# The output of all eight token tiles is summed in PSUM banks by TensorE, the residual rows included; the squares and the final product read the banks

## The reference

```python
def reference(x, ...):
    ...
    x = x + gt1 * hybrid_mixer(h, ...)
    h = rmsnorm(x, g_norm2[l]) * (1.0 + sc2) + sh2
    x = x + gt2 * moe(h, router_w, router_b, exp_w1[l], exp_w3[l], exp_w2[l])
    return rmsnorm(x, g_final)

def moe(h, ...):
    ...
    out = jnp.einsum('nk,nkd->nd', weights, y_assign)   # two expert rows per token, weighted

def rmsnorm(x, g):
    y = x * lax.rsqrt(jnp.mean(x * x, axis=-1, keepdims=True) + EPS)
    return y * g
```

## Time and profile before

| what | us |
|---|---|
| time, median of 3 runs | 1066.58 (1065.75 to 1068.83) |
| the profiled execution, its own time | 1064.69 |
| its span | 1062.9 |
| last expert product ends, from the span's start | 1013.5 |
| first tile of expert rows is there | 1023.6 |
| last `finish` ends | 1058.65 |

### The profile page before, as it was taken

One profiled execution on the slowest core, in us unless ns is written; L12 is line 12 of the kernel. 1 busy time (PEld: TensorE's weight loads), 2 busy tenths in 40 slices (PEclk: granted clock), 3 DMA queues, 4 the chain that ended last, 5 costly groups with the idle time before them and its releaser, 6 DMA issues.

```text
span 1062.9 us, 12951 instructions
## 1 busy us (share of the span) xinstructions
PE 982.5 (92%) x5014; PEld 675.1 (64%) x5014; DVE 546.6 (51%) x858; ACT 353.8 (33%) x525; POOL 133.7 (13%) x130
## 2 busy tenths in 40 slices
PE   3799999999999999985899999999999999999853
PEld 2478988888889688874664755656475565545321
DVE  2589734514663356654773546447354554625126
ACT  4521124422223443331743424243251422522022
POOL 1100000001210001113122202222220020210001
PEclk9899999999999999995899999999999999999977
DMA  9838611111203272428999999999999999999975
GB/s 367 290 124 308 249 41 40 40 40 41 98 24 140 84 291 101 119 90 266 326 359 390 403 428 427 427 425 429 426 426 427 427 426 426 427 426 428 406 302 220
DMA packets 52319, 295.82 MB, mean 278 GB/s; under 512 B 10889, under 2 KB 23194, under 8 KB 35874
## 3 DMA queue, kind: packets, MB, share of 16 engines
q1 hardware_dynamic: 43682, 274.00, 65.1%
q0 software_dynamic: 7424, 16.80, 4.1%
q10 hardware_dynamic: 1152, 4.19, 1.0%
HBM read 278.03 MB, written 25.33 MB: 285 GB/s over the span
## 4 chain that ended last, share of the span: by engine, by line
PE 77%; DMA 10%; DVE 6%; ACT 2%; issue 1%; DVEq 1%; POOL 1%; ACTq 0%; SPq 0%; POOLq 0%
PE bank L1151 9%; PE bank L1132 8%; DMA place_dt_float<-in_exp_w_dram 8%; PE bank L1127 5%; PE bank L1121 5%; PE bank L1157 4%; PE bank L1124 4%; PE bank L822 4%; PE bank L824 4%; PE bank L823 4%; PE bank L827 4%; PE bank L828 4%; PE bank L829 4%; PE bank L996 2%; PE bank L999 2%; PE bank L1002 2%
## 5 line engine op out<-in xcount | busy, mean ns | idle before, releaser
L1428 ACT CAST place_dt_float32r<-place_dt_float 128x4096 fp32r<-128x4096 f32 x32 | 115.7, 3615 | 128.6 <-DMA place_dt_float<-in_exp_w_dram 99.8
L1988 DVE TENSOR_TENSOR place_dt_float32r<-place_dt_float,place_dt_float32r 128x4096 fp32r<-128x4096 f32 x32 | 141.4, 4417 | 26.6 <-ACT place_dt_float32r L1428 26.6
L1151 PE MATMUL bank<-place_dt_float,arena 128*128 128x512 f32 x256 | 113.7, 597 | 0.8 <-issue 0.8
L1132 PE MATMUL bank<-place_dt_float,tail_dt_float 128*64 128x512 f32 x512 | 113.4, 595 | 0.0
L723 POOL DMA_INDIRECT y_dram<-arena,slot_i x24 | 61.0, 2543 | 411.7 <-DVE arena L1999 392.6
L827 PE MATMUL bank<-low_r 128*128 128x256 f32 (+1 forms) x320 | 93.8, 293 | 0.0
L829 PE MATMUL bank<-low_r 128*128 128x256 f32 (+1 forms) x320 | 90.8, 284 | 0.0
L828 PE MATMUL bank<-low_r 128*128 128x256 f32 (+1 forms) x320 | 90.7, 284 | 0.0
L641 POOL TENSOR_TENSOR stats<-stats,half 128x1 f32<-128x1 f32 (+1 forms) x34 | 26.3, 775 | 460.8 <-DVE stats L1480 434.0
L1151 PEld LDWEIGHTS bank<-place_dt_float,arena 128*128 128x128 f32 x256 | 47.3, 190 | 56.0 <-issue 54.6
L1132 PEld LDWEIGHTS bank<-place_dt_float,tail_dt_float 128*64 128x64 f32 x512 | 35.3, 137 | 72.8 <-issue 72.8
(11 more groups left out here) (272 smaller groups left out, 1536.5 us busy)
## 6 DMA issues: line engine op xcount, KB each, us to landing
place_dt_float<-in_exp_w_dram SPq DMA_DIRECT2D x96, 2048.0 KB, 23.4
arena<-in_w_ada_dram SPq DMA_DIRECT2D x24, 1024.0 KB, 9.2
low<-in_w_in_dram SPq DMA_DIRECT2D x11, 1024.0 KB, 5.5
arena<-y_dram SPq DMA_DIRECT2D x8, 1024.0 KB, 7.4
arena<-in_x_dram SPq DMA_DIRECT2D x2, 2048.0 KB, 12.2
wout_dt_float<-in_w_out_dram SPq DMA_DIRECT2D x2, 2048.0 KB, 7.8
arena<-in_x_dram SPq DMA_DIRECT2D x8, 512.0 KB, 3.6
x_dram<-arena SPq DMA_DIRECT2D x8, 512.0 KB, 2.6
```

Source lines behind the costliest of these rows:

```text
L1132: mm = pe.matmul(out_[rows_, :], x[:, k, rows_], w[:, k, :], start=(k == 0), stop=(k == KD - 1))
L1151: mm = pe.matmul(bank[5 + j][:], hT_sb[:, k, :], ws[0][:, k, cols], start=(k == 0), stop=(k == KF - 1))
L1428: act.copy(part_hi[0 if kind == "w1" else 1], alias[F32][n % SLOTS]).then_inc(S["w_hi"], 1)
L1988: TT(alias[F32R][n], alias[F32][n], part_hi[j].bitcast(F32), ALU.subtract).then_inc(S["w_lo"], 1)
```

## The change

PE now forms the whole output of all eight tiles in the banks. `residual(t)` puts the residual rows there with an identity matrix as the stationary operand (two products of 128x512, the first of their banks' sums); the four products with the routing weights are added to them. Tile t uses banks 2*(t%4) and 2*(t%4)+1, so four tiles are under way at once. The residual products of tiles 0 to 3 stand ahead of everything else; that of tile t+1, for tiles 4 to 7, stands behind the products of tile t and waits until tile t-3 is finished. ACT squares the two halves straight from the banks, each with its own sum. DVE adds the two sums (and EPS) in one small instruction and multiplies the banks by the norm and `gfin` into `acc`, in two halves. DVE's passes over the expert rows and its additions of the banks are gone. `w_diag` now has 16 matrices in place of 10.

```diff
-        by_pe = (1, 2, 3, 5, 6)
-        w_diag = F.take(len(by_pe), 2, P)
+        w_diag = F.take(TILES, 2, P)
+        out_bank = lambda t, h: bank[2 * (t % 4) + h]
+        ss_half = mv
...
+            def residual(t):
+                wait(pe, S["fin_out"], t - 3)
+                for h in range(2):
+                    pe.matmul(out_bank(t, h)[:], ident, acc[:, t, h * HT:(h + 1) * HT], start=True, stop=False)
+
+            pe.wait_ge(S["y_ready"], PASSES)
+            pe.wait_ge(S["early_ld"], 32)
+            for t in range(4):
+                residual(t)
             pe.wait_ge(S["h2_act"], TILES + 1)
-            for n, t in enumerate(by_pe):
+            for t in range(TILES):
                 pe.wait_ge(*y_landed(t))
-                if n >= 2:
-                    pe.wait_ge(S["fin_acc"], by_pe[n - 2] + 1)
                 for h in range(2):
                     for k in range(2):
-                        mm = pe.matmul(bank[2 * (n % 2) + h][:], w_diag[:, n, k, :], yy[:, t, k * D + h * HT:k * D + (h + 1) * HT],
-                                       start=(k == 0), stop=(k == 1))
+                        mm = pe.matmul(out_bank(t, h)[:], w_diag[:, t, k, :], yy[:, t, k * D + h * HT:k * D + (h + 1) * HT],
+                                       start=False, stop=(k == 1))
                 mm.then_inc(S["out_mm"], 1)
+                if 4 <= t + 1 < TILES:
+                    residual(t + 1)
...
             for t in range(TILES):
-                act.wait_ge(S["fin_acc"], t + 1)
-                act.activation(sq_junk, acc[:, t, :], ACT.Square, accum_out=ssf[:, t:t + 1])
+                act.wait_ge(S["out_mm"], 2 * TILES + t + 1)
+                for h in range(2):
+                    act.activation(sq_junk[:, h * HT:(h + 1) * HT], out_bank(t, h)[:], ACT.Square, scale=D ** -0.5,
+                                   accum_out=ss_half[:, t, h:h + 1])
                 act.drain().then_inc(S["fin_ss"], 1)
                 if t:
                     store(t - 1)
...
-            def mean_of_tile(t):
+            for t in range(TILES):
                 dve.wait_ge(S["fin_ss"], t + 1)
-                mean_sq(ssf[:, t:t + 1], msf[:, t:t + 1], D, S["fin_ms"])
-
-            def finish(t):
+                STT(msf[:, t:t + 1], ss_half[:, t, 0:1], EPS, ss_half[:, t, 1:2], ALU.add, ALU.add).then_inc(S["fin_ms"], 1)
                 dve.wait_ge(S["fin_rs"], t + 1)
-                STT(acc[:, t, :], acc[:, t, :], rsf[:, t:t + 1], gfin, ALU.mult, ALU.mult).then_inc(S["fin_out"], 1)
-
-            for t in range(TILES):
-                if t in by_pe:
...
+                for h in range(2):
+                    cols = slice(h * HT, (h + 1) * HT)
+                    ins = STT(acc[:, t, cols], out_bank(t, h)[:], rsf[:, t:t + 1], gfin[:, cols], ALU.mult, ALU.mult)
+                ins.then_inc(S["fin_out"], 1)
```

More of the change, by code:

```diff
@@ L168, in build @@
         ss1, ms1, rs1 = (stat(TILES) for _ in range(3))
-        ssf, msf, rsf = ss1, ms1, rs1
+        msf, rsf = ms1, rs1
         mv = stat(2 * TILES).rearrange("p (t two) -> p t two", two=2)
@@ L387, in build @@
                   "ov_sil", "ov_hid", "ov_htr", "ov_hT", "ov_y", "ov_ysb", "ov_sc", "ov_free", "gp_passed", "dve_passed",
-                  "early_ld", "fin_acc", "fin_ss", "fin_ms", "fin_rs", "fin_out"):
+                  "early_ld", "fin_ss", "fin_ms", "fin_rs", "fin_out"):
             S[n] = sem(n)
@@ L1202, in _ @@
                     mm.then_inc(S["ov_y"], 1)
+                pe.wait_ge(S["ov_ysb"], OVER)
+            def residual(t):
[6 more added lines that the diff above has]
+                residual(t)
             pe.wait_ge(S["h2_act"], TILES + 1)
-            for n, t in enumerate(by_pe):
+            for t in range(TILES):
                 pe.wait_ge(*y_landed(t))
-                if n >= 2:
-                    pe.wait_ge(S["fin_acc"], by_pe[n - 2] + 1)
                 for h in range(2):
                     for k in range(2):
-                        mm = pe.matmul(bank[2 * (n % 2) + h][:], w_diag[:, n, k, :], yy[:, t, k * D + h * HT:k * D + (h + 1) * HT],
-                                       start=(k == 0), stop=(k == 1))
+                        mm = pe.matmul(out_bank(t, h)[:], w_diag[:, t, k, :], yy[:, t, k * D + h * HT:k * D + (h + 1) * HT],
+                                       start=False, stop=(k == 1))
                 mm.then_inc(S["out_mm"], 1)
+                if 4 <= t + 1 < TILES:
+                    residual(t + 1)
         @block.scalar
@@ L1442, in _ @@
             act.wait_ge(S["y_mm"], PASSES)
-            for n, t in enumerate(by_pe):
+            for t in range(TILES):
                 for k in range(2):
-                    ins = act.activation(w_diag[:, n, k, :], ident, ACT.Identity, scale=top_w[:, t, k:k + 1])
+                    ins = act.activation(w_diag[:, t, k, :], ident, ACT.Identity, scale=top_w[:, t, k:k + 1])
             ins.then_inc(S["h2_act"], 1)
```

## The result

The changed kernel takes 1070.47 us (median of 20 runs, 1067.62 to 1073.04), the kernel before 1066.12 us in the same series. The ratio is 1.0041, 95% interval 1.0032 to 1.0050: slower by 4.4 us (3.4 to 5.3). The forecast was 1071.2 us and 0.43%.

A forecast was written before the change was run, and what follows sets the result against it. DVE's loop bounds the tail before, PE after: start 1024.8, plus 34.3 us of products, 0.24 us and 3.96 us puts the last `finish` at 1063.3, 4.6 us later: 1071.2 us, 0.43% slower, range 1068.5 to 1073.6.

The forecast's parts named there:

- The bound: Tail from about 1036 us: DVE and its loop with ACT and POOL set the pace before; PE after the change.
- The price of a product: PE's products in the tail: 0.858 us each at full clock, 0.429 us for each of two records; 40 take 34.3 us.
- Rival D: PE's records follow each other faster in a long run; below 0.371 us the kernel is faster, at 0.248 us 1055.6; chance 0.06.
- Rival E: Residual products of tiles 4 to 7 cost nothing, taking 6.9 us off: 2.3 us faster, 1064.3 us; chance 0.10.
- The start: PE's first eight residual products wait for the gain vector until 1016.2, take 6.9 us plus 1.7 us, and end at 1024.8.
- the half clock: PE's start on the residual products: half speed for 3.4 us, costing 1.7 us.
- rival B: First residual products run at full clock or end by 1023.64, saving 1.2 us: 3.4 us slower, 1070.0 us; chance 0.22.
- A: The forecast itself: PE bounds the tail, with half clock for 3.4 us at its start; 1071.2 us; chance 0.50.
- Behind PE: Steps after PE's last product: two squares 1.4 us, read to `finish` 1.26 us, `finish` 1.3 us; together 3.96 us.
- The 0.24 us: Delay between the end of PE's last product at 1059.1 and ACT seeing it at 1059.3.
- The sum: End of the tail: last `finish` at 1063.3 instead of 1058.65, 4.6 us later; on the median 1066.58 this gives 1071.2 us.
- the hold of ACT's queue: Kernel before, ACT's first store: 1.76 us on the chain at 1037.66, read as the end of a longer hold.

The follow-up runs named there:

- `own_sem`: Changed kernel with the last norm's gain vector on its own semaphore, so PE's first residual products wait for the residual rows alone: 1069.05 us, ratio 1.0051; again 1069.03 us, 1.0027.
- the third series: Last four kernels on one chip: changed kernel again (1071.60 us), gain vector on its own semaphore, five added products before the residuals, and the kernel before with later stores.
- `filler`: Changed kernel with five more identity products behind PE's last expert product, to keep PE busy until the residual products: 1069.17 us, ratio 1.0024; again 1069.89 us, 1.0037.

## Why the prediction was right

**The bound.** It was read as DVE and its loop before and PE after. Both are shown: 8.5 us of DVE work cost 5.5 us before (a stretch of 40.6 against 35.0) and nothing after (38.15 in both), and four tiles' residual products done twice cost 6.5 us.

**The price of a product.** 0.858 us, taken from two DVE starts 3.43 us apart, held for the 40 products from tile 0 on: the changed kernel's chain has 1.72, 3.43 and 13.73 us for four, eight and 32 records. The 34.3 us from tile 0 to the last product are there to the tenth (1027.28 on the chain to 1061.62 in the timeline). Rival D is out: over 80 records the spacing stayed at 0.429 us. The Trainium skill has two figures for this, in "TensorE: Matmul & The Clock Gate", section "Back-to-back issue gap". If a record is two passes, which no run here shows, the measured spacing agrees with the isolated gap of some 216 ns for each pass and not with the sustained 131 ns. Rival E is out: the late residual products cost their full price.

**The start.** This is the term that was sized worst. It was put at 1024.8 us, 1.2 us behind tile 0's landing. In the changed kernel's first profile PE goes on to tile 0 only at 1027.28: the gain vector landed at 1017.75, not 1016.2, since it was issued 1.56 us later than in the kernel before (988.47 against 986.91), and the half clock took 4.6 us, not 3.4. Tile 0's rows, 10.1 us behind the last expert product as elsewhere, would by an estimate have let PE go on at about 1023.7, so this start costs 3.6 us. In the four profiles of variants with the same wait it costs nothing (rival B): PE stood still for 2.5 to 2.9 us, about as long as the forecast had it, but went on at full clock. Single executions thus show 3.6 us (A, longer than forecast) or nothing (B), and none the 1.2 us of the forecast. In the median the comparison with `own_sem` in the third series prices the start at 2.6 us. One reading of the rows was wrong besides: the residual rows were said to land at 1011.9, 4.3 us before the gain vector, while in the three profiles with a semaphore each they land only 1.2 us before it. So the vector that PE does not read holds it for no more than that. The 2.6 us in the median are more; the half clock that can follow a later start would account for the rest, but no run isolates it.

**Behind PE.** 3.96 us were forecast, 3.54 us measured from ACT's start. The 0.24 us that the forecast put ahead of it are not there either, since ACT starts 0.03 us after PE's last product; they appear where PE comes out of a wait (13.97 us for 32 records in `own_sem`, 13.73 in the changed kernel), which is why the two stretches are 38.15 and 37.9 us. The two squares took 1.26 us (1061.65 to 1062.91), not 1.4, and `finish` 1.41, not 1.3. The rest is a misreading: the 1.26 us between ACT's read and `finish` in the earlier trace rows held 0.4 us in which DVE was still in the `finish` of tile 6. In the changed kernel nothing is ahead of DVE there, and it is 0.87 us.

**The sum.** The measured parts are 38.15 - 35.0 = 3.15 us for the stretch and 2.6 us for the start, 5.8 us. The ratios say 4.4 us (3.4 to 5.3) and, in the third series, 5.5 us (4.2 to 7.0). The forecast of 4.6 us lies in both intervals, with the start 1.4 us too cheap and the end 0.4 us too dear. Between the two profiled executions the difference is larger: 1071.09 - 1064.69 = 6.4 us, which is 2.9 us for the stretch and 3.6 us for the start. So who sets the pace and what a product costs were right by reasoning; that the median came within 0.2 us of the 4.6 us is in part luck, since the start has two sizes in the six profiles that have it and the forecast named one between them. One thing was seen in the rows and not weighed: the hold of ACT's queue was part of the kernel before's 35.0 us. Against that kernel with later stores the change would be another 2.7 us slower, by its ratio.

## What to carry to other kernels

When work moves from one engine to another, count the receiver's instructions at the spacing that its own rows show, and find the point from which it, not the giver, sets the end. Here that point was (35.0 - 0.24 - 3.54) / 0.858 = 36 products behind the first landing: with 40 the kernel lost, with 32 it was level or a little ahead, and with 28, two tiles left to DVE and the gain vector on its own semaphore, it won 5.7 us. Work that needs none of the late data is free only as long as it starts early enough: look at which landing it really waits for. And a step's price read from the last tile of a pipeline holds the work of the tile before it.

## What the runs showed of the hardware that was not expected

- The landing of the residual rows reads as 23 to 25 us after the issue where they share a semaphore with the gain vector, and as 27.8 to 28.5 us where they have their own, while that of the gain vector stays at 28.6 to 29.4 us. I read this as the profile not telling two transfers apart that count on one semaphore; the 4 MB of residual rows and the 512 KB of the gain vector then land 1.2 us apart.
- The same start of PE ran at 2.4 GHz in some executions and at 1.2 GHz in others. In the profiles of the changed kernel and its variants pauses of 1.4 to 2.9 us were followed by the full clock and pauses of 3.15 and 4.3 us by the half clock. Where it came, it lasted 4.6 to 6.2 us from PE's start, and the 16 records took 9.4 to 10.2 us in place of 6.9. In the three profiles with a slow start the last expert products had run at full clock (7.09 us for 32 records); in the others, `filler` apart, they had begun at half clock (8.7 to 8.8 us). That sets the length of the pause: in all six profiles with the shared semaphore and no filler PE went on with the residual products 11.3 to 11.6 us after the last expert products began, so the 1.7 us that these took less, PE stood still longer. Whether the length of the pause or the clock before it decides the clock behind it no run separates.
- POOL's power takes 1.51 us in the kernel before when DVE's second pass of tile 4 or 7 runs beside it, and 0.54 us otherwise; in the changed kernel it is 0.54 us for all eight tiles (mean 787 ns before, 543 ns after). This agrees with the Trainium skill, "SBUF — State Buffer", section "SBUF: two separate sides", by which a DVE operation with two inputs in SBUF and a GpSimd operation that reads SBUF shut each other out. In the kernel before this is on the chain: twice `finish` waited for POOL, 0.43 and 0.44 us, so by an estimate from these rows at most 0.9 us of its 35.0 us. In the changed kernel only the last tile's power is on the path.
- The first store held ACT's queue for 4.98 us in the kernel before and for 4.73 us in its variant with more DVE work, for 1.61 us where it came later, and for 0.38 to 0.41 us in every profile of the changed kernel and its variants. The loads of the expert rows were running or just done in all of them. Why is open.
